# One recurrence, reordered: strict products, lane work and the right side change places on four engines

## The reference

```python
def rwkv7_scan(r, decay, k, v, kk, a, s0, reverse):
    def step(S, inp):
        r_t, w_t, k_t, v_t, kk_t, a_t = inp
        sa = jnp.einsum('bhvk,bhk->bhv', S, -kk_t)
        S = (S * w_t[:, :, None, :] + sa[..., None] * (kk_t * a_t)[:, :, None, :]
...
```

## Time and profile before

| | us |
|---|---|
| median of 3 runs | 2242.22 |
| lowest, highest | 2237.65, 2248.16 |
| the profiled execution | 2246.36 |
| its span in the trace | 2244.5 |
| PE busy (share of the span) | 2108.7 (94%) |
| VectorE, ScalarE, GpSimd busy | 850.5, 750.8, 921.5 |
| chain that ended last: PE's share | 83% |

### The profile page before, as it was taken

How to read it: one execution, slowest core, us unless ns; L and a number is a source line. 1 busy time by engine, 2 the same in 40 slices (tenths; PEclk the granted TensorE clock), 3 DMA queues, 4 the chain that set the end, 5 groups by cost and what they waited for, 6 DMA issues and landing times.

```text
span 2244.5 us, 30591 instructions
## 1 busy us (share of the span) xinstructions
PE 2108.7 (94%) x12951; PEld 1691.0 (75%) x12951; DVE 850.5 (38%) x1278; ACT 750.8 (33%) x1090; POOL 921.5 (41%) x423
## 2 busy tenths in 40 slices
PE   5999999989996798998999999899999989989997
PEld 2677877868844677766778778677888868988996
DVE  3323032162267555336230321632123156446123
ACT  1522122263343122246221221622222266456343
POOL 0434443444406011044334434343444435447884
PEclk9999999999998788889999999999999999999998
DMA  9563446223201333232643363356232222324551
GB/s 327 161 213 131 141 134 228 92 82 112 94 20 24 76 77 72 81 113 87 222 160 123 118 219 117 102 170 212 85 106 82 94 71 96 113 74 141 182 174 71
DMA packets 226631, 280.31 MB, mean 125 GB/s; under 512 B 37589, under 2 KB 192227, under 8 KB 226180
## 3 DMA queue, kind: packets, MB, share of 16 engines
q1 hardware_dynamic: 223706, 273.36, 37.1%
q10 hardware_dynamic: 2794, 5.04, 0.6%
HBM read 267.90 MB, written 10.49 MB: 124 GB/s over the span
## 4 chain that ended last, share of the span: by engine, by line
PE 83%; DVE 7%; ACT 4%; DMA 3%; issue 2%; SPq 1%; ACTq 0%; POOL 0%; POOLq 0%; DVEq 0%
PE psum L1153 82%; DMA arena<-inverse_kept 1%; DVE rs L1980 1%; DMA arena<-in_ada_w 1%; DMA arena<-in_x 1%; DMA inverse_kept<-h 1%; ACT arena L805 1%; DVE h L1959 1%; ACTq L717 0%; DVE h L2242 0%; ACT L867 0%; PE psum L1527 0%; DVE arena L2181 0%; DVE arena L2068 0%; DVE h L2234 0%
## 5 line engine op out<-in xcount | busy, mean ns | idle before, releaser
L2454 POOL TENSOR_TENSOR w_lo<-arena,w_hi 128x1024 fp32r<-128x1024 f32 x332 | 814.3, 2458 | 1026.4 <-ACT w_hi L776 1024.2
L1153 PE MATMUL psum<-u_hi,w_hi 128*128 128x512 f32 (+1 forms) x1888 | 699.0, 370 | 38.5 <-ACT u_hi L805 15.2
L1153 PE MATMUL psum<-u_hi,w_lo 128*128 128x512 f32 (+1 forms) x1888 | 689.6, 365 | 0.0
L1153 PE MATMUL psum<-u_lo,w_hi 128*128 128x512 f32 (+1 forms) x1888 | 675.2, 363 | 0.0
L776 ACT ACTIVATE w_hi<-arena 128x1024 fp32r<-128x1024 f32 x332 | 349.2, 1058 | 737.1 <-PE psum L1153 726.1
L1153 PEld LDWEIGHTS psum<-u_hi,w_hi 128*128 128x128 f32 x1888 | 363.0, 192 | 129.7 <-issue 28.8
L1153 PEld LDWEIGHTS psum<-u_hi,w_lo 128*128 128x128 f32 x1888 | 363.4, 192 | 55.1
L1153 PEld LDWEIGHTS psum<-u_lo,w_hi 128*128 128x128 f32 x1888 | 359.3, 191 | 53.4 <-issue 0.5
L1153 PE MATMUL psum<-arena 64*64 64x64 f32 (+12 forms) x3140 | 292.8, 295 | 37.1 <-DMA arena<-inverse_kept 13.8
L1153 PEld LDWEIGHTS psum<-arena 64*64 64x64 f32 (+5 forms) x3140 | 210.0, 168 | 111.8 <-issue 56.1
L1929 DVE TENSOR_TENSOR tmp<-psum,tmp 128x512 f32<-128x512 f32 (+1 forms) x88 | 54.9, 624 | 586.9 <-ACT tmp L830 586.9
(11 more groups left out here) (268 smaller groups left out, 1476.4 us busy)
## 6 DMA issues: line engine op xcount, KB each, us to landing
arena<-in_ada_w SPq DMA_DIRECT2D x48, 1536.0 KB, 6.8
arena<-in_ffn_wg SPq DMA_DIRECT2D x44, 1024.0 KB, 5.4
arena<-in_ffn_wu SPq DMA_DIRECT2D x44, 1024.0 KB, 7.9
arena<-in_ffn_wd SPq DMA_DIRECT2D x20, 2048.0 KB, 8.8
arena<-in_ev_w_in SPq DMA_DIRECT2D x6, 2048.0 KB, 7.7
arena<-in_od_w_in SPq DMA_DIRECT2D x6, 2048.0 KB, 8.1
arena<-in_ffn_wd SPq DMA_DIRECT2D x4, 1024.0 KB, 4.9
arena<-in_ev_w_out SPq DMA_DIRECT2D x2, 2048.0 KB, 9.7
```

The lines of the kernel that those rows point to most:

```text
L1153: return pe.matmul(dst, w, x, start=first_, stop=last, skip_group_check=True)
L2454: pool.tensor_tensor(piece_shape(split_lo(pc), src), src, piece_shape(split_hi(pc).bitcast(F32), src), ALU.subtract).then_inc(S("lo_done"), 1)
```

## The change

Six edits, all in the recurrence of the first layer:

1. On PE `right_side(gi - 1)` stands ahead of `widen_z(gi, 4)` in each group, and on ScalarE their copies (`right_side_out`, `z_out(gi, 4)`) change places with it.
2. In groups 2 and 4 both strict products, and on VectorE both of their takes, stand ahead of the previous group's outputs; before, the second one stood behind them.
3. The lane work of levels 4 and 8, and its end, stand together ahead of the first doubling mask in groups 1, 3 and 5; before, level 8 stood behind it.
4. `lane_pairs` for chunks 2 and 3 is done in groups 2 and 4, behind the first mask of the rest; before, it was done in groups 3 and 5. For chunk 1 it stays in group 1.
5. The rates are made in slices: that of the first chunk first, the other slices behind the takes of the first strict products; `hyena_out(1)` goes behind them.
6. GpSimd waits for the end of the first lane work before it makes the slots of the second chunk.

```diff
@@ ScalarE
                     j, hf = gi // 2, gi % 2
-                    z_out(gi, 4)
                     if hf == 0 and 0 < j < 3:
                         decays_of(j + 1, 0, 0, 5)
                     if gi:
                         right_side_out(gi - 1)
+                    z_out(gi, 4)
@@ PE
-                    widen_z(gi, 4)
                     if gi:
                         right_side(gi - 1)
+                    widen_z(gi, 4)
                     widen(gi, 4)
                     if gi:
                         solve(gi - 1)
                     widen_z(gi, 5)
                     if ahead:
                         strict(gi + 2)
+                        strict(gi + 3)
                     if gi:
                         outputs(gi - 1)
-                    if ahead:
-                        strict(gi + 3)
@@ VectorE
-                def rates(d):
-                    ve.wait_ge(S("kd_f"), 4 * (d + 1))
-                    ve.scalar_tensor_tensor(out=rate[d], in0=rate[d], scalar=-1.0, in1=kk, op0=ALU.mult,
+                def rates(d, from_, to):
+                    r = three(rate[d])[:, :, from_ * P:to * P]
+                    ve.scalar_tensor_tensor(out=r, in0=r, scalar=-1.0, in1=three(kk)[:, :, from_ * P:to * P], op0=ALU.mult,
...
-                rates(1)
-                rates(0)
+                ve.wait_ge(S("kd_f"), 8)
+                for d in range(2):
+                    rates(d, chunk_of(d, 0), chunk_of(d, 0) + 1)
...
                 take_strict(0)
+                rates(0, 1, 4)
+                rates(1, 0, 1)
+                take_strict(1)
+                rates(1, 2, 4)
+                ve.wait_ge(S("ve_steps"), v.n)
                 hyena_out(1)
-                take_strict(1)
...
+                    ahead = hf == 0 and 0 < j < 3
+                    if gi == 1:
+                        lane_pairs(1)
                     if hf and j < 3:
-                        lane_pairs(j + 1)
                         lane_level(4)
+                        lane_level(8)
+                        lanes_out()
                     double(gi, 4)
                     if gi:
                         take_solution(gi - 1)
-                    if hf and j < 3:
-                        lane_level(8)
-                        lanes_out()
-                    if hf == 0 and 0 < j < 3:
+                    if ahead:
                         take_strict(gi + 2)
+                        take_strict(gi + 3)
                     if gi:
                         take_outputs(gi - 1)
-                    if hf == 0 and 0 < j < 3:
-                        take_strict(gi + 3)
...
+                    if ahead:
+                        lane_pairs(j + 1)
                     take_rest(gi, 1)
@@ GpSimd
                     else:
                         pool.wait_ge(S("rates"), 1)
+                        pool.wait_ge(S("lanes"), 1)
```

## The result

The changed kernel takes **2253.65 us** (median of 4 runs, 2251.56 to 2256.17), the kernel before 2239.93 beside it (4 runs, 2236.27 to 2248.16): ratio 1.0051, 95% interval 1.0032 to 1.0070. It is slower by about half a percent. The time lies just inside the range, 0.35 us under its upper end, and 11 us above the forecast. It is outside the band of the forecast itself (E, 2236 to 2249), and it lies where the prediction had put a chance of 0.14 (over 2253.4).

The account below looks back on a forecast made before the run. PE's queue and waits were taken to bound the kernel: the recurrence's loop through memory, then half clock at even groups. Terms (a) to (f) gave -1.6 us, (g) +2.0: +0.4, so 2242.6 us; range 2225 to 2254.

Parts of the forecast that it names:

- E: Whole kernel: the forecast itself comes true, 2236 to 2249 us; chance 0.50.
- (f): Pairs in groups 2 and 4: new wait of some 0.7 us for lane blocks; +1.8 us, bounds 0 and +6.
- (g): PE's clock falls at all 7 group starts, 2.85 us each: 20 us against 18 before, +2 us.
- the signs that would show it wrong: Recurrence: full clock in even groups and end 15 us earlier, half clock at odd starts, or VectorE waiting over 1.5 us.
- (a): First lane work: GpSimd waiting removes VectorE's slow rows, so the first doubling starts sooner; -4.1 us, bounds -4.9 and +0.8.
- Rival D: First lane work: GpSimd is not what slowed it; (a) becomes +0.8, 2247.5 us; chance 0.08.
- (b): Rates made in slices on VectorE: bring nothing at their own place; 0, at most +0.5 us.
- (c): Three even groups: right side ahead of the first doubling product covers the wait for the transfer; -2.9 us.
- (d): Four odd groups: with the right side ahead PE stands 1.4 instead of 0.36 us; +4.8 us, bounds +4 and +6.
- (e): Groups 2 and 4: both strict products ahead of the outputs take VectorE's second take off the path; -1.2 us.
- rival C: Clock falls already in the pause at all seven starts, 5.5 us each; 2261 us, slower; chance 0.10.
- Rival B: Clock holds with no transfer waited for; only two falls of 1.5 us remain; 2225.6 us; chance 0.20.

Follow-up runs that it names:

- e4: Kernel before with only GpSimd's wait for the first lane work added: 2238.7 us, ratio 0.9989 to the kernel before.
- e9: Kernel before plus GpSimd's wait, level 8 lane work ahead of the doubling, and both strict products ahead of the outputs: 2228.2 us, ratio 0.9919.
- e7: Kernel before with only the second half of the lane work moved ahead of the doubling on VectorE: 2235.5 us, ratio 0.9969.
- e11: Changed kernel with four unused matmuls filling PE's pause before each right side and pairs back in odd groups: 2225.6 us, ratio 0.9916 to the kernel before.
- e12: e9 plus two unused 128x128 matmuls in PE's pause ahead of each first doubling product: 2219.6 us, ratio 0.9889 to the kernel before.
- e8: Kernel before with only both strict products and their takes ahead of the outputs in groups 2 and 4: 2242.1 us, ratio 0.9993.
- e2: Changed kernel with the pairs moved back to the start of the odd groups: 2244.3 us, ratio 1.0013 to the kernel before.
- e6: Changed kernel with four unused 128x128 matmuls in PE's pause ahead of each right side: 2241.4 us, ratio 0.9996 to the kernel before.
- e3: Changed kernel with first doubling product ahead of the right side again and pairs back in odd groups: 2232.0 us, ratio 0.9957 to the kernel before.
- e1: Changed kernel with the first doubling product ahead of the right side again on PE and ScalarE: 2240.6 us, ratio 0.9981 to the kernel before.

## Why the prediction was right or wrong

The direction of the change's parts was mostly right, and the sum was 11 us too low, from two terms, (f) and (g). That the time still lies in the range is luck: the range ran far past the forecast's own band, to 2254, for a share of the case "(f) and (g) both go badly", and that case came. Of the signs that would show it wrong, two came true (VectorE waits for over 1.5 us in groups 2 and 4; half clock over most of the odd groups' starts), and the recurrence grew by 8.0 us where 6 was the limit.

**(a) GpSimd waits: right.** Forecast -4.1 us; the first doubling comes 4.5 us sooner in the changed kernel and 3.9 with this edit alone, and the slow rows are gone in both. Rival D falls with e4.

**(b) Slices: right so far as shown.** Nothing is lost without them (e9).

**(c) and (d) Right side ahead: the size was right for the kernel as a whole, the cause of (c) was put in the wrong place.** At an unchanged clock I had +1.9 us for both: -2.9 from covering the transfer and +4.8 from the odd starts. The pauses are as I read them, 1.43 us. But the cover isn't the right side's doing: the lane work moved ahead hides the transfer alone, and is worth 7.0 us by itself (e7). With the transfer hidden, the right side ahead costs time at even starts as well as at odd ones (1.4 and 0.8 us in groups 2 and 4, 0.9 and 0.5 in 1 and 5), by estimate 7.5 us in all (e11 against e12). The sum hid that, beside the lane work moved ahead, this edit was pure loss.

**(e) Both strict products ahead: not shown either way** (e8), 1.2 us is below what can be measured.

**(f) The pairs: wrong in size.** I took 7.7 us from the issue of the store to the data, from the first round, and so a wait of 0.7 us and +1.8 in all. It was 9.8 us and waits of 3.26 and 3.59 us on VectorE; undoing it gives 8.5 us (e2). Its upper bound of +6 was drawn for "a transfer that takes 2 us longer", and that is what happened; 6.4 us of idle PE, the rest at the clock. The step that failed is the one that took a transfer's time from a round in which its two stores lay 3.5 us apart. The change itself pushed them to 1.2 us apart (part e, as e8 shows) and onto the load of `tu`.

**(g) The clock: mechanism right, size wrong.** It fell at all seven starts, as forecast; in five out of the pause of 1.4 us joined to the right side, in two behind the wait for the pairs, which (g) did not have (without that wait they come at the right side, too: e2). I took a fall *late* in the right side, 2.85 us each. It came within 1 us behind the right side's first matmul in four of the seven, and in two before it (813 and 875 us); one came late (936). How I read the cost: the second mask of the widening stands at 794.06 in group 2, 11.4 us behind the start of the right side at 782.69. In e6, with a short fall, it is 789.89 - 781.47 = 8.4; at full clock it would be 7.2, from the 5.96 of the earlier trace rows without the product, its 1.15 and 0.1 for the bare copy; it is 7.20 in e6 at the starts of groups 6 and 7, where the clock doesn't fall. So 4.2 us a start, 4.7 in two, 1.2 in the last:

```profile
794.06 0.43 DVE L2201 COPY_PREDICATED arena<-masks,psum 128x256 f32<-128x256 uint8 x1 [0.54 <-PE psum L1153]
```

Seven starts give some 27 us, not 20: 3.9 a start, not far from the 4.4 at which rival C would have decided. C's reading (the fall in the pause already) was the nearer one. That filling the pause alone gives 12.3 us back (e6) shows that a large part of this cost is real and comes from the pause.

Put together for the two profiled executions: -4.5 (a), +1.9 (c, d), -1.2 (e), +6.4 (f, PE's idle time) and +9 (g, 27 less 18) give +11.6; (c), (d) and (e) are the forecast's own numbers here. The recurrence grew by 8.0. The difference is 3.6 us, and 3.2 of it lie in group 0, which no term had: before, the clock was at half from 754 to 761 us, after it was full from 743 to 755, and the last mask of group 0 ends 50.4 us behind VectorE's first slot instead of 58.1, 7.7 us gained where (a) has 4.5. The tail behind the last pause, too, is 1.3 us shorter (963.09 to 972.40 against 956.25 to 966.86), with 6.8 us at half instead of 10.2; so the other terms together are 0.9 us too low. That between the medians the loss is larger (11.4 us by the ratio) is the spread: the profile of before lies 4 us over its median, that of after 2 us under its own.

Rival B (the clock holds, since no transfer is waited for) is refuted for the changed kernel. The Trainium skill's account (TensorE: Matmul & The Clock Gate, "HAM oscillation - how this bites in real kernels") puts the falls down to PE waiting for DMA between bursts of matmuls. Here the trace of e2 has seven falls in, or up to 3.5 us behind, pauses of 1.43 us in which PE waits for one mask on VectorE, and no row of PE at these starts waits for a DMA. That e11, with the waits gone and the pauses filled, comes out at the 2225.6 us that B had is an accident: it took two more edits, and the clock is at half for 37.6 us there all the same.

## What to carry to other kernels

Take a change of several moves apart before judging it: here four moves together give 0.4% (e3) and three of them 0.8 (e9), two others cost 0.9 to 1.3%, and the forecast of the sum was "no change". When the clock falls at a short pause in which PE waits for another engine, count the slow time behind it (here 4.2 us for a pause of 1.4), prefer the order that leaves the shorter pause, and if the pause stays, try filling it with unused matmuls of about its length. A transfer's time taken from one round holds only while its neighbours in the queue keep their distance.

## What the runs showed of the hardware

Adding matmuls that nothing uses made the kernel faster, by 12 us (e6), and in another order likely by 9 (e12), with no other edit. A fill on a quarter of the array did as well as one on all of it (ratios 1.0000 and 0.9996). And the clock fell 2.8 us behind a pause of only 0.38 us, too, and stayed at half for 13.7 us (e3). One and the same kernel took 2228 or 2245 us on the same chip, with mean granted clocks of 0.968 and 0.960 (e1), so a gain of half a percent needs many executions to be seen.

GpSimd's multiplies had slowed VectorE's small copies 3.5 times (2.68 against 0.77 us) with hardly any loss of their own: GpSimd's product takes 1.26 to 1.40 us beside them and 1.26 alone. VectorE's smallest operations lost most. Those of 128x8 behind the two copies took 1.12 to 1.20 us (L2257 at 728.79 us: 1.19) against 0.17 in the changed kernel: seven times as long, and about the length of one of GpSimd's products.
